# Hybrid decoder trunk on one core: expert down products in four column groups, small products in halves

## The reference, cut to what matters

```python
for l in range(DEPTH):                       # DEPTH = 2
    h = rmsnorm(x, attn_norm[l])
    proj = h @ w_in[l]
    ...                                      # four mixers, each 256 columns wide
    x = x + mix @ w_out[l]
    h = rmsnorm(x, ffn_norm[l])
    if l % 2 == 0:
        x = x + swiglu(h, ffn_w1, ffn_w3, ffn_w2)          # width 2816
    else:
        x = x + moe_swiglu(h, router, moe_w1, moe_w3, moe_w2)
return rmsnorm(x, final_norm)

def moe_swiglu(h, router, w1, w3, w2):       # 8 experts of width 1408, top 2
    ...
    for e in range(N_EXPERTS):
        out = out + combine[..., e:e + 1] * swiglu(h, w1[e], w3[e], w2[e])
    return out
```

## Time and profile before

| | |
|---|---|
| median of 3 runs | 1142.22 us |
| the profiled execution | 1143.13 us |
| its span, first to last instruction | 1141.3 us |
| granted TensorE clock, mean | 0.982 of 2.4 GHz |
| PE busy | 1102.5 us |
| PEld busy | 837.2 us |
| DVE, ACT, POOL busy | 285.3, 192.9, 61.4 us |
| bytes moved by DMA | 213.34 MB |

### The profile page before, as it was taken

One profiled execution on the slowest core, in us unless ns is written; L12 is line 12 of the kernel. 1 busy time (PEld: TensorE's weight loads), 2 busy tenths in 40 slices (PEclk: granted clock), 3 DMA queues, 4 the chain that ended last, 5 costly groups with the idle time before them and its releaser, 6 DMA issues.

```text
span 1141.3 us, 22432 instructions
## 1 busy us (share of the span) xinstructions
PE 1102.5 (97%) x9790; PEld 837.2 (73%) x9790; DVE 285.3 (25%) x645; ACT 192.9 (17%) x444; POOL 61.4 (5%) x67
## 2 busy tenths in 40 slices
PE   8999999899999999999999969999999999999996
PEld 6887887488888543887789549595949494949592
DVE  4432473500000001233376341020111112021112
ACT  2244231100000001214323011011010111101011
POOL 2000411000000000000312100000000000000000
PEclk8999999999999999999999989999999999999998
DMA  9633101335554445343210256989898989899870
GB/s 325 196 122 105 43 1 38 111 117 160 160 159 167 156 148 155 119 135 109 74 38 1 74 185 203 343 279 351 287 344 289 343 293 323 305 301 332 279 272 37
DMA packets 168650, 213.34 MB, mean 187 GB/s; under 512 B 5120, under 2 KB 151200, under 8 KB 168480
## 3 DMA queue, kind: packets, MB, share of 16 engines
q1 hardware_dynamic: 166032, 210.29, 56.0%
q10 hardware_dynamic: 2576, 2.45, 0.7%
HBM read 211.67 MB, written 1.05 MB: 186 GB/s over the span
## 4 chain that ended last, share of the span: by engine, by line
PE 95%; DVE 3%; issue 1%; ACT 1%; POOL 0%; DMA 0%; DVEq 0%; POOLq 0%; ACTq 0%
PE bank L518 93%; PE bank L523 1%; DVE tok L1434 1%; POOL small L1343 0%; DMA x_sb<-in_x 0%; DVE b_att L1616 0%; DVE b_q L1413 0%; PE bank L1045 0%; DVE x_sb L1410 0%; PE bank L829 0%; ACT tok L1121 0%; DVE small L1425 0%; ACT hT L1133 0%; DVE hT L1410 0%; PE bank L797 0%
## 5 line engine op out<-in xcount | busy, mean ns | idle before, releaser
L518 PE MATMUL bank<-hT,ring 128*128 128x256 f32 (+1 forms) x1184 | 260.3, 382 | 0.0
L518 PEld LDWEIGHTS bank<-hT,ring 128*128 128x128 f32 (+1 forms) x1184 | 223.4, 189 | 36.1 <-issue 2.7
L518 PEld LDWEIGHTS bank<-region_m,ring 128*64 128x64 f32 x4096 | 170.3, 137 | 8.6 <-issue 8.6
L518 PE MATMUL bank<-region_m,ring 128*64 128x96 f32 x4096 | 173.7, 246 | 2.9 <-DVE region_m L1860 1.6
L518 PE MATMUL bank<-ring,region_e 128*96 128x512 f32 (+1 forms) x368 | 160.0, 594 | 0.0
L518 PEld LDWEIGHTS bank<-ring,region_e 128*96 128x96 f32 (+1 forms) x368 | 64.1, 176 | 89.5 <-issue 88.5
L518 PE MATMUL bank<-ring,hT 128*128 128x256 f32 (+1 forms) x448 | 127.8, 442 | 1.4 <-ACT hT L1138 1.4
L518 PE MATMUL bank<-region_e 128*128 128x128 f32 (+2 forms) x512 | 119.2, 384 | 0.0
L1410 DVE TENSOR_TENSOR region_e<-region_f,bank 128x96 f32<-128x96 f32 (+1 forms) x110 | 31.7, 288 | 341.7 <-ACT region_f L1318 198.9
L518 PEld LDWEIGHTS bank<-ring,hT 128*128 128x128 f32 x448 | 84.0, 190 | 35.7 <-issue 25.8
L518 PEld LDWEIGHTS bank<-region_e 128*128 128x128 f32 (+1 forms) x512 | 71.9, 191 | 46.9 <-issue 46.8
(11 more groups left out here) (234 smaller groups left out, 715.0 us busy)
## 6 DMA issues: line engine op xcount, KB each, us to landing
ring<-in_moe_w SPq DMA_DIRECT2D x80, 1024.0 KB, 6.9
region_e<-in_moe_w SPq DMA_DIRECT2D x40, 1024.0 KB, 6.8
ring<-in_ffn_w SPq DMA_DIRECT2D x33, 1024.0 KB, 5.4
ring<-in_w_in SPq DMA_DIRECT2D x22, 1024.0 KB, 5.4
ring<-in_w_out SPq DMA_DIRECT2D x8, 1024.0 KB, 4.9
ring<-in_moe_w SPq DMA_DIRECT2D x16, 512.0 KB, 5.8
region_e<-in_moe_w SPq DMA_DIRECT2D x8, 512.0 KB, 4.0
ring<-in_w_in SPq DMA_DIRECT2D x2, 1088.0 KB, 5.5
```

The source lines that it names most:

```text
L518: return nc.tensor.matmul(o, lhsT, rhs, start=start, stop=stop, skip_group_check=True)
```

## The change

Three edits.

1. `down_round`: an expert's down products are cut into products of 32 slots (weight columns) by 256 streamed columns. Four of them, one for each group of 32 partitions of the output, make a round; three rounds cover the 96 slots and 1024 columns of one chunk: 132 products in place of 22. The fourth group takes the last 256 columns of one third of the slots in each round, so its results stand in partitions 96 to 127 of banks 2 and 3 and are copied to their place by two further copies on ScalarE and one on VectorE. The last two `w2` pieces (`TAIL`) are worked through round by round, and both are released at the end.
2. `SCATTER` is reordered: both products that need the lower half of `slot_y` come first; the waits use two new semaphores.
3. `mm_halves` issues a product as two halves of 64 weight columns, and the small products of the mixers and the router now use it. Where the kernel had such halves already (gather and up products), the code is rewritten with the helper and issues the same products.

```diff
@@ expert_released
-                elif k < E_PIECES - 1:
-                    sp.wait_ge(sem("moe_w2_used"), i * (UP2 - 1) + k - 2 * UP2 + 1)
+                elif k < E_PIECES - TAIL:
+                    sp.wait_ge(sem("moe_w2_used"), i * (UP2 - TAIL) + k - 2 * UP2 + 1)
@@ tensor
+            def mm_halves(o, lhsT, rhs, start=False, stop=False):
+
+                for q in range(0, P, HALF):
+                    last = mm(o[q:q + HALF, :], lhsT[:, q:q + HALF], rhs, start=start, stop=stop)
+                return last
@@ one of the small products; CO, GO, AO, RH, U, Y, BON and RT likewise
-                    mm(o[:, c], a_pt[:, s, :], a_v[:, 0, v], start=(s == 0), stop=True)
+                    mm_halves(o[:, c], a_pt[:, s, :], a_v[:, 0, v], start=(s == 0), stop=True)
@@ experts, down
+                    def down_round(k, r):
+
+                        w = w2_rows(k)
+                        for g in range(4):
+                            a, c = (g, r) if g < 3 else (r, 3)
+                            o = banks[2 + r // 2][g * QUARTER:(g + 1) * QUARTER, (r % 2) * GW:(r % 2 + 1) * GW]
+                            last = mm(o, slot_act[:, k, a * QUARTER:(a + 1) * QUARTER], w[:, c * GW:(c + 1) * GW],
+                                      start=(k == 0 and r != 1), stop=(k == UPC - 1))
+                        return last
+
                     for k2 in range(UP2):
...
-                        for half in range(2):
-                            for kk in range(m):
-                                k = 2 * k2 + kk
-                                last = mm(banks[2 + half][0:CAP, :], slot_act[:, k, :],
-                                          w[:, kk, half * 512:(half + 1) * 512], start=(k == 0), stop=(k == UPC - 1))
-                            if k2 == UP2 - 1:
-                                last.then_inc(full[2 + half], 1)
-                        if k2 < UP2 - 1:
+                        for k in range(2 * k2, min(2 * k2 + 2, UPC)):
+                            pe.wait_ge(free[k % 2], nth(i, k % 2, k // 2 + 1))
+                        if k2 < UP2 - TAIL:
+                            for k in (2 * k2, 2 * k2 + 1):
+                                for r in range(3):
+                                    last = down_round(k, r)
                             last.then_inc(sem("moe_w2_used"), 1)
+                    for r in range(3):
+                        for k in range(2 * (UP2 - TAIL), UPC):
+                            last = down_round(k, r)
+                        if r:
+                            last.then_inc(full[1 + r], 1)
@@ experts, scatter
-                        pe.wait_ge(free[2 + half], nth(i, 2 + half, 2 - half))
-                        if b > 3:
+                        if half == 0:
+                            pe.wait_ge(sem("moe_y_low"), i + 1)
+                        else:
+                            pe.wait_ge(sem("moe_y_high"), 2 * i + 2)
+                        if b == 2:
+                            pe.wait_ge(free[2], nth(i, 2, 2))
+                        elif b == 3:
+                            pe.wait_ge(free[3], nth(i, 3, 1))
+                        else:
                             pe.wait_ge(free[b], nth(i, b, 0))
@@ scalar
-                        nc.scalar.copy(slot_y[:, 0:512], banks[2][0:CAP, :]).then_inc(free[2], 1)
+                        nc.scalar.copy(slot_y[:, 0:512], banks[2][0:CAP, :]).then_inc(sem("moe_y_low"), 1)
+                        nc.scalar.copy(slot_y[0:QUARTER, 768:1024], banks[2][CAP:P, 0:GW])
+                        nc.scalar.copy(slot_y[QUARTER:2 * QUARTER, 768:1024],
+                                       banks[2][CAP:P, GW:2 * GW]).then_inc(free[2], 1)
+                        act.wait_ge(free[2], nth(i, 2, 2))
+                        act.sem_inc(sem("moe_y_high"), 1)
@@ vector
-                        v.tensor_copy(slot_y[:, 512:1024], banks[3][0:CAP, :]).then_inc(free[3], 1)
+                        v.tensor_copy(slot_y[:, 512:768], banks[3][0:CAP, 0:GW])
+                        v.tensor_copy(slot_y[2 * QUARTER:CAP, 768:1024], banks[3][CAP:P, 0:GW]).then_inc(free[3], 1)
+                        dve.wait_ge(free[3], nth(i, 3, 1))
+                        v.sem_inc(sem("moe_y_high"), 1)
-SCATTER = ((4, 0, 0), (5, 0, 1), (2, 1, 0), (3, 1, 1))
+SCATTER = ((4, 0, 0), (5, 1, 0), (2, 0, 1), (3, 1, 1))
```

More of the change, by code:

```diff
@@ L15 @@
 HALF = 64
+QUARTER = 32
+TAIL = 2
 D = 1024
@@ L666, in layer_mixers @@
                     for j in range(2):
-                        last = mm(bank("BON", l)[:, t * 4 + 2 * j:t * 4 + 2 * j + 2],
+                        last = mm_halves(bank("BON", l)[:, t * 4 + 2 * j:t * 4 + 2 * j + 2],
                                   d_rk[:, j * SEQ + t * P:j * SEQ + (t + 1) * P], const("head_sel"),
@@ L683, in layer_mixers @@
                     o = bank("CO", l)
-                    mm(o[:, h * HD:(h + 1) * HD], a0[:, hh, 0:P], c_v[:, 0, v], start=(h == 0), stop=True)
-                    mm(o[:, GW + h * HD:GW + (h + 1) * HD], a0[:, hh, P:SEQ], c_v[:, 0, v])
-                    last = mm(o[:, GW + h * HD:GW + (h + 1) * HD], a1[:, h, :], c_v[:, 1, v], stop=True)
+                    mm_halves(o[:, h * HD:(h + 1) * HD], a0[:, hh, 0:P], c_v[:, 0, v], start=(h == 0), stop=True)
+                    mm_halves(o[:, GW + h * HD:GW + (h + 1) * HD], a0[:, hh, P:SEQ], c_v[:, 0, v])
+                    last = mm_halves(o[:, GW + h * HD:GW + (h + 1) * HD], a1[:, h, :], c_v[:, 1, v], stop=True)
                 fills(last, "CO", l)
@@ L737, in b_output @@
                     for h in range(4):
-                        mm(o[:, t * GW + h * HD:t * GW + (h + 1) * HD], b_att[:, t, h, :],
-                           b_v[:, t, h * HD:(h + 1) * HD], start=(t == 0 and h == 0), stop=True)
+                        mm_halves(o[:, t * GW + h * HD:t * GW + (h + 1) * HD], b_att[:, t, h, :],
+                                  b_v[:, t, h * HD:(h + 1) * HD], start=(t == 0 and h == 0), stop=True)
                 pe.wait_ge(sem("gla_state"), l + 1)
@@ L866, in solve @@
                 for h in range(4):
-                    last = mm(bank(f"U{c}", l)[:, h * HD:(h + 1) * HD], inv[c]["Tt"][:, h * P:(h + 1) * P],
+                    last = mm_halves(bank(f"U{c}", l)[:, h * HD:(h + 1) * HD], inv[c]["Tt"][:, h * P:(h + 1) * P],
                               d_rh[:, c, h * HD:(h + 1) * HD], start=(h == 0), stop=True)
@@ L875, in tile_output @@
                     s = slice(h * HD, (h + 1) * HD)
-                    mm(o, lg[:, c, h, P:256], d_u[:, c, s], start=(h == 0))
-                    last = mm(o, mg[:, c, h, P:256], d_v[:, c * GW + h * HD:c * GW + (h + 1) * HD], stop=(c == 0))
+                    mm_halves(o, lg[:, c, h, P:256], d_u[:, c, s], start=(h == 0))
+                    last = mm_halves(o, mg[:, c, h, P:256], d_v[:, c * GW + h * HD:c * GW + (h + 1) * HD], stop=(c == 0))
                     if c == 1:
-                        last = mm(o, ar[:, h // 2, h % 2, 1, P:256], d_s[:, h // 2, :], stop=True)
+                        last = mm_halves(o, ar[:, h // 2, h % 2, 1, P:256], d_s[:, h // 2, :], stop=True)
                 fills(last, f"Y{c}", l)
@@ L980, in experts @@
                             wait_features(("F0", "F1", "F2", "F3"), l, k)
-                        last = mm(bank("RT", l)[:, t * N_EXPERTS:(t + 1) * N_EXPERTS], hT[:, k, t * P:(t + 1) * P],
+                        last = mm_halves(bank("RT", l)[:, t * N_EXPERTS:(t + 1) * N_EXPERTS], hT[:, k, t * P:(t + 1) * P],
                                   router_sb[:, k, :], start=(t == 0 and k == 0), stop=(k == KC - 1))
@@ L1002, in gather @@
                             for t in range(NT):
[L1003 to L1007, removed]
+                                last = mm_halves(banks[6 + h][:, c * CAP:(c + 1) * CAP],
+                                                 tok[:, t, (4 * h + c) * P:(4 * h + c + 1) * P], pick[:, t, :],
+                                                 start=(c == 0 and t == 0), stop=(t == NT - 1))
                         last.then_inc(full[6 + h], 1)
@@ L1035, in experts @@
                                 for k in range(KC):
[L1036 to L1039, removed]
+                                    last = mm_halves(banks[b][:, f * CAP:(f + 1) * CAP], w[:, k, jj * P:(jj + 1) * P],
+                                                     slot_h[:, k, :], start=(f == 0 and k == 0), stop=(k == KC - 1))
                             last.then_inc(full[b], 1)
```

17 lines of the change are left out of this document (8 added, 9 removed).

## The result

| | before | after |
|---|---|---|
| median of all runs beside each other | 1142.41 us | 1166.37 us |
| lowest to highest (4 runs) | 1139.45 to 1143.24 | 1163.42 to 1168.79 |
| ratio, 95% interval | | 1.0213 [1.0179, 1.0247] |
| profiled execution, its span | 1143.13, 1141.3 | 1163.42, 1161.2 |
| granted TensorE clock, mean | 0.982 | 0.955 |

The change makes the kernel 24 us slower; the forecast was 1150 us, 8 slower.

What follows compares the result with a forecast made beforehand. TensorE's stream was taken to bound the kernel. From the profiled 1143.1 us, less 37 (down), 1 (scatter) and 6 (small products), plus 52 (instruction fetches), gave 1151, by the median 1150 us; range 1096 to 1185.

Steps and rivals of the forecast that it cites:

- Down: Expert's down products: four column groups side by side, 14.5 us instead of 19.13, saving 37 us in all.
- The second rival: Down products: groups run only two by two, 29.0 us per expert, 1215 us without fetches; chance 0.13.
- Scatter: Scatter after the down products: extra copies hidden, 3.5 us, about 0.1 us saved per expert, 1 us in all.
- Small products: Mixer and router products in halves: 3 to 13 us less together, 6 taken.
- my two bounds: Time of a side-by-side pair of 64-column halves in the small products: 57 to 85 ns.
- changes of form: Switches between whole and halved array at the small products: 0.1 us each, 36 of them, 3.6 us.
- The loop's code: Expert loop on TensorE: body grows to ten instruction blocks, refetched at each branch back, costing 52 us.
- The first rival: Expert loop: ten blocks fit, or overwritten ones cost nothing; 1098 us by the median, chance 0.22.
- Price per branch: Loop's branch back: 7.4 us for each of seven, from 1 to 15.
- first hole: PE standing still after the scatter at the branch back: 2.9 us left open after 2.6 covered by scatter passes.
- The first term: Block fetch at the loop's branch back, beside running transfers: 5.5 us, from a range of 1 to 7.
- The clock term: Up products after the branch back: clock at 0.50 for 3.4 us, loses 1.7, taken as 2.0 us.

Runs made afterwards that it cites:

- mix_head0: Kernel before with the small products of mixers and router in halves and the expert loop's head at the start of a block: 1132.19 us, ratio 0.9913.
- place 144: Kernel before with only TensorE's loop head moved, to 144 instructions into a 256-instruction block: 1175.35 us, ratio 1.0272.
- place 200: Kernel before with only TensorE's loop head moved, to 200 instructions into a 256-instruction block: 1191.99 us, ratio 1.0445.
- nine_fit2: Changed kernel with nine down products per chunk, whole gather and last up products, loop head at a block's start, seven blocks: 1119.93 us, ratio 0.9788.

## Why the prediction was right, and where it was too small

The mechanism is the one that was forecast, and the time is 16 us off. That it lies in the range of 1096 to 1185 says little, since the range runs from 4% faster to 4% slower; what was at stake is that the loop's code costs more than the down products give, and that was given 0.54.

**Down, right.** 66 rounds of 0.220 us, 14.5 us, came as 14.38. The 264 passes would take 58.1 us one after the other in the whole array, so four groups gain 4.04 times. The second rival (two by two, 29 us) is out. The Trainium skill has 2.38 times for three column tiles in "TensorE: Matmul & The Clock Gate", Part 3, and 3.07 for four row tiles; an estimate by these puts the part at 18.9 us or more, and the measurement decides against both as a steady ratio for four column groups. Scatter was forecast at 3.5 and takes 3.70 us, so that down and scatter save 37 us in all, for 38.

**Small products, too small.** I took 6 us of 3 to 13, `mix_head0` measured 9.9. (In the profiled executions the first up pass starts 9.3 us earlier than before in `mix_head0` and 12.7 in the changed kernel.) `AO` is the row to look at, 24 passes in 2.79 us before, about 110 ns each; in the timeline of the changed kernel it is now 48:

```profile
170.81 1.62 PE L520 MATMUL bank<-region_m,hT 128*64 128x64 f32 x48
```

A pair of halves thus takes about 60 ns ((1.62 less one pass's tail of 0.22) over 47, times 2), near the lower of my two bounds (57) and not near the 85 of the 96-column pair that I took as the nearest row. 288 passes at 50 ns less (110 less 60) are 14.4 us, and less the 3.6 that I had for changes of form 11, against 9.9. The term failed because it took the row's value instead of scaling it by the columns, which the same sentence had done for the bound.

**The loop's code, right in kind.** Packets, a hole by "issue" behind each scatter, 0.50 behind it: all three were named, and the runs show them as cause, not company: the same loop costs 50 us more or nothing, by where its head stands. The first rival (ten blocks fit, 1098 us) is out. Of the Trainium skill's two rules in "Runtime: NRT & Kernel Launch", "Instruction fetch mechanics", the size (2048 instructions, the next block fetched ahead) agrees with a seven-block loop that stays and with the eight blocks held at place 144; that there are only two cache lines does not, since trips without a packet are in six kernels here. Read as "whatever is under 2048 fits", which is how I used it for the 1,690, the size misleads as well: 1,690 from place 200 do not stay.

**Price per branch, too small.** Forecast 7.4 us: 2.9 first hole, 2.0 second, 2.0 clock, 0.5 later. Measured, as means of seven: 4.84, 2.01, 3.3 and, of 10.3 in all, 0.1 for the rest. The first term was 5.5 us from branch to first pass; it is 6.9 to 7.3. The estimate of "about 7 us" for a block stood in the same paragraph, from the hole at 716.19, and I cut it to 5.5 without a row for it. The clock term assumed a single 3.4 us at 0.50; with two holes it stood there for 6.8 to 13.7 us in a trip. Together 72 us for 52.

**The sum.** Less 37, less 10, plus 72 is +25, measured +24.0. As forecast: less 38, less 6, plus 52, +8. The two mis-sized terms have opposite signs and lie 20 and 4 us off, so that 4 us of the first were hidden by luck; the price of the branch carries the miss.

The same section of the Trainium skill also says that a taken branch to a place outside the current two-page window stops the engine until the block is there. The trace agrees in what it shows of the changed kernel (a branch of 6.4 to 6.6 us) and disagrees for the kernel before, whose branch goes back by six blocks in 0.21 us.

## What to carry to other kernels

Count the instructions of a hardware loop in blocks of 256 from where its head stands, before making its products smaller: here seven blocks were free and eight or more cost 7 to 10 us per trip (4 on average at place 144), mostly more than the 4.7 us that four column groups gave. An edit far from the loop, in code that gets faster by itself, can move the head and lose more than it gains; fix the head's place, then judge the edit. If a change wants more instructions than fit, look for the same concurrency in larger pieces (512 columns, whole products where they cost least), as in `nine_fit2`.

## What was not expected of the hardware

- The branch's own duration shows the miss: 0.21 us when its target is in the store, 4.3 us (median) when it is not and the DMA engines are idle, 6.6 us (median) in the changed kernel beside weight transfers at some 350 GB/s.
- The store holds eight blocks, but one goes to the block fetched ahead: an eight-block loop pays in every second trip (place 144) or in each (place 200).
- The second hole, some 50 instructions after the first, is there at a DMA share of 0.21 and lasts 2.0 us, with an instruction packet under way from 796.21 us: it is the delay of one more fetch, and a head at the start of a block removes it.
- Four column groups ran at 54 ns per 256-column pass, each with its own weight load, a quarter of the 0.220 us of a whole-array pass.
